# Attention stage of a two-layer backbone: a third buffer of probabilities, and another order of work on the scalar and the vector engine

## Chip, cores and metric

The kernel runs on one core of one Trainium2 chip. The metric is the device time of one execution in microseconds (us); the time given for a kernel is the median of its runs. The engines are named as in the profile: PE (TensorE, matrix multiplies; PEld is its loading of weights), ACT (ScalarE), DVE (VectorE), POOL (GpSimd), SP (SyncE, which issues most DMAs). Each engine works through its own queue of instructions in order. An instruction can wait until a semaphore has reached a value, and then everything behind it on the same engine waits too.

## The reference, cut to what matters

The program computes two layers over 512 latent tokens with 256 context tokens, width 1024, in fp32. Layer 0 is attention with 8 query heads and 2 key/value heads of width 128 and then a squared-ReLU MLP; layer 1 is a Hyena long convolution and an MLP. Only the attention is touched:

```python
def gqa_attend(q, k, v):
    s = jnp.einsum('bqkgd,bskd->bkgqs', q, k).astype(jnp.float32) * (q.shape[-1] ** -0.5)
    p = jax.nn.softmax(s, axis=-1).astype(v.dtype)
    return jnp.einsum('bkgqs,bskd->bqkgd', p, v)
...
    k_all = jnp.concatenate([k_l, k_c], axis=1)     # 512 latent + 256 context keys
    v_all = jnp.concatenate([v_l, v_c], axis=1)
    o = lax.map(lambda qblk: gqa_attend(qblk, k_all, v_all), qb)   # 4 blocks of 128 queries
```

## The kernel before, in words

Every large product is made at nearly fp32 accuracy from three faster products: each operand is split into a high part (a copy in the rounded format fp32r) and a low part (value minus high part), and `mm3` (L1430 to L1434) adds high times high, high times low and low times high. So each operand costs a copy on ACT (high part) and a subtraction on DVE (low part).

The attention is cut into NQ = 32 tiles: 8 heads times 4 blocks of 128 queries, each against NK = 768 keys. Each engine has its own loop over steps n, and a step works on several tiles at once, each at another stage of its life. With the names used below, step n holds:

- On PE (L1583 to L1610), in this order: **T(n-3)**, six 128x128 transposes of the normalised probabilities of tile n-3 into PSUM (L1589); **S(n)**, the scores of tile n, two `mm3` of 512 and 256 columns; and at odd n from 5 on **PV**, `prob_values((n-5)/2)`, 18 matmuls of 256 columns that multiply two tiles of turned probabilities with the values.
- On ACT (L774 to L800): at even n from 6 on **O**, the high part of the attention output, which waits for PV (L778); **H(n-3)**, the high part `phi` of the turned probabilities, which waits for T(n-3) (L785); and **B(n-1)** and **E(n-1)**, a small scaling of the negated row maximum (L794) and the exponential from PSUM into `PROB`, with the row sums into `rsum` (L795). They wait for the maximum of tile n-1, and for the transposes of the tile that used this buffer of `PROB` before.
- On DVE (L1190 to L1216): **R(n-2)** and **N(n-2)**, the reciprocal of the row sum and the normalisation of the probabilities in place (L1196, L1197), which wait for E(n-2); **L(n-3)**, the low part `plo` of the turned probabilities, which waits for H(n-3) (L1202); **M(n)**, the row maximum of the scores of tile n, which waits for S(n) (L1208); at even n from 6 on the low part of the attention output (L1181); and at n = 3, 7, 11, ... one row of the modulation product of 128x1024 elements (**A**, L1187), 8 in all.

Scores and turned probabilities share three double banks of PSUM in rotation. `score(n)` is double bank (2n+1) mod 3 and `turned(m)` is 2(m+3) mod 3, so T(n-3) is written where the scores of tile n-2 were, and S(n) where the turned probabilities of tile n-4 were. PE therefore has these waits ahead of T(n-3) and S(n):

```python
                    pe.wait_ge(p_done, m + 1)               # m = n - 3: N(n-3)
                    pe.wait_ge(exp_done, min(n - 1, NQ))    # E(n-2) has read the scores
                    ...
                    if n >= 4:
                        pe.wait_ge(plo_done, n - 3)         # L(n-4) has read the turned tile
```

`PROB` has two buffers in `scratch` (`S[:, 0:2]` and `S[:, 2:4]`), used by tile number modulo 2.

Of the kernel before, what the change touches and what calls it, by code (L numbers as in the profile page):

```python
# [27 lines left out]
ALU = mybir.AluOpType  # L28
ACT = mybir.ActivationFunctionType
AX = mybir.AxisListType  # L30

P = 128
# [4 lines left out]
NK = NT + NC  # L37
# [51 lines left out]
def build(nc, xT, ctxT, cT, cols, wpack, ahead, apack, fw1, fw2, fw3, featsT, decay, tables, consts, ropes, fdram, out):  # L89
    with ExitStack() as ctx:  # L90
        def sb(name, shape, dt=F32, stack=ctx):
            return stack.enter_context(nc.sbuf_tensor(name, shape, dt))

        def sem(name):
            return ctx.enter_context(nc.semaphore(name))
# [14 lines left out]
        S = sb("scratch", [P, 12, NT])  # L110
# [5 lines left out]
        gain = sb("gain", [P, 2, 4, KC])  # L116
        gainc = sb("gainc", [P, KC])
        nmax = sb("nmax", [P, 2])
        rsum = sb("rsum", [P, 2])
        rinv = sb("rinv", [P, 2])  # L120
        asum = sb("asum", [P, ADA_QUARTER])
        qg = sb("qg", [P, 1])
        rq = sb("rq", [P, NH * QT])
        bmax = sb("bmax", [P, 2])
        epst = sb("eps", [P, 1])
        tap2 = sb("tap2", [P, 2, NT])
        ident, ones = (cst[:, n, :] for n in range(2))
# [108 lines left out]
        rq_done = sem("rq_done")  # L236
# [11 lines left out]
        score_done = sem("score_done")  # L248
        nmax_done = sem("nmax_done")
        exp_done = sem("exp_done")  # L250
        rinv_done = sem("rinv_done")
        p_done = sem("p_done")
        pt_done = sem("pt_done")
# [81 lines left out]
        def spread(a):  # L335

            return TRIO[a % 3][:, :, :].rearrange("p a b -> p (a b)")[:, 0:NK]

        def score(n):

            return spread(2 * n + 1)

        def turned(m):

            return spread(2 * (m + 3))
# [6 lines left out]

        XH = [S[:, 4 + j % 4, :] for j in range(KC)]
        YC = [y[:, j, :] for j in range(KC)]
        PROB = [S[:, 2 * n:2 * n + 2, :].rearrange("p a b -> p (a b)")[:, 0:NK] for n in range(2)]

        FP, FP_, FQ, FQ_ = (araw[:, n // 2, n % 2 * NT:(n % 2 + 1) * NT] for n in range(4))
        UNIT_RAW = (es[:, 0, :], tap2[:, 0, :])
# [8 lines left out]
        NQ = NH * QT  # L367
# [7 lines left out]
        def f(ap):  # L375
            return ap.bitcast(F32)
# [261 lines left out]
        def _(act):  # L638
            own = Own(act, own_act)
            A = nc.scalar.activation  # L640
# [133 lines left out]
            for n in range(NQ + 5):  # L774
                if n >= 6 and n % 2 == 0:
                    m = (n - 6) // 2
                    act.wait_ge(pv_done, m + 1)
                    A(hhi[:, m // 2, (m % 2) * 2 * P:(m % 2 + 1) * 2 * P], (B2, B3)[m % 2][:, 0:2 * P],  # L778
                      ACT.Copy).then_inc(ohi_done, 1)
                m = n - 3  # L780
                if 0 <= m < NQ:
                    act.wait_ge(pt_done, m + 1)
                    if m >= 4:
                        act.wait_ge(pv_done, m // 2 - 1)
                    A(phi[:, m // 2 % 2, :, (m % 2) * P:(m % 2 + 1) * P],  # L785
                      turned(m).rearrange("p (b c) -> p b c", b=KT), ACT.Copy).then_inc(phi_done, 1)
                m = n - 1
                if 0 <= m < NQ:
                    act.wait_ge(nmax_done, m + 1)
                    if m >= 2:  # L790
                        act.wait_ge(pt_done, m - 1)
                    if m == 0:
                        act.wait_ge(rq_done, 1)
                    own(A(bmax[:, m % 2:m % 2 + 1], nmax[:, m % 2:m % 2 + 1], ACT.Copy, scale=rq[:, m:m + 1]))  # L794
                    A(PROB[m % 2], score(m), ACT.Exp, bias=bmax[:, m % 2:m % 2 + 1], scale=rq[:, m:m + 1],  # L795
                      accum_out=rsum[:, m % 2:m % 2 + 1]).then_inc(exp_done, 1)
                if n == 1:
                    act.wait_ge(csum_done, 1)
                    A(crow[:, 0:NT], B2[:, :], ACT.Copy).then_inc(crow_done, 1)
                    A(crow[:, NT:2 * NT], B3[:, :], ACT.Copy).then_inc(crow_done, 1)  # L800
# [112 lines left out]
            for k in range(4):  # L913
                z_hi(k)
                n = 4 * (k + 1)
# [47 lines left out]
        def _(dve):  # L963
            own = Own(dve, own_dve)
            TT = nc.vector.tensor_tensor
            STT = nc.vector.scalar_tensor_tensor
            TS = nc.vector.tensor_scalar
# [135 lines left out]
            for q in range(4):  # L1103
                for ft in range(2):
                    n = 4 * q + 2 * ft
# [72 lines left out]
            def o_lo(m):  # L1178
                dve.wait_ge(ohi_done, m + 1)
                cols_ = slice((m % 2) * 2 * P, (m % 2 + 1) * 2 * P)  # L1180
                TT(hlo[:, m // 2, cols_], (B2, B3)[m % 2][:, 0:2 * P], f(hhi[:, m // 2, cols_]), ALU.subtract).then_inc(olo_done, 1)  # L1181

            def ada_row(k, loads, dst, early=False):

                dve.wait_ge(arow_in[k], 16 * loads)
                slot = arow_slot(k, early)
                nc.vector.tensor_tensor_reduce(slot, slot, crow if early else crow1[:, :], 1.0, 0.0, ALU.mult, ALU.add,  # L1187
                                               dst).then_inc(arow_done, 1)

            for n in range(NQ + 5):  # L1190
                m = n - 2
                if 0 <= m < NQ:
                    dve.wait_ge(exp_done, m + 1)
                    if m >= 2:
                        dve.wait_ge(p_done, m - 1)
                    own(nc.vector.reciprocal(rinv[:, m % 2:m % 2 + 1], rsum[:, m % 2:m % 2 + 1]))  # L1196
                    TS(PROB[m % 2], PROB[m % 2], rinv[:, m % 2:m % 2 + 1], None, ALU.mult).then_inc(p_done, 1)  # L1197
                m = n - 3
                if 0 <= m < NQ:
                    dve.wait_ge(phi_done, m + 1)  # L1200
                    at = slice((m % 2) * P, (m % 2 + 1) * P)
                    TT(plo[:, m // 2 % 2, :, at], turned(m).rearrange("p (b c) -> p b c", b=KT),  # L1202
                       f(phi[:, m // 2 % 2, :, at]), ALU.subtract).then_inc(plo_done, 1)
                if n < NQ:
                    dve.wait_ge(score_done, n + 1)
                    if n >= 2:
                        dve.wait_ge(exp_done, n - 1)
                    nc.vector.tensor_reduce(out=nmax[:, n % 2:n % 2 + 1], in_=score(n), op=ALU.max,  # L1208
                                            axis=AX.X, negate=True).then_inc(nmax_done, 1)
                if n >= 6 and n % 2 == 0:  # L1210
                    o_lo((n - 6) // 2)
                if n < NQ and n % 4 == 3:
                    r = n // 4
                    if r == 0:
                        dve.wait_ge(crow_done, 2)
                    ada_row(r % ADA_RING, r // ADA_RING + 1, mods[:, 16 + r:17 + r], True)  # L1216
# [156 lines left out]
            for k in range(5):  # L1373
# [4 lines left out]
                n = 4 * (k + 1)  # L1378
# [48 lines left out]
        def _(pe):  # L1427
            mm = nc.tensor.matmul

            def mm3(o, lh, ll, rh, rl, first, last):  # L1430

                mm(o, lh, rh, start=first, stop=False)  # L1432
                mm(o, lh, rl, start=False, stop=False)  # L1433
                return mm(o, ll, rh, start=False, stop=last)  # L1434
# [148 lines left out]
            for n in range(NQ + 4):  # L1583
                m = n - 3
                if 0 <= m < NQ:
                    pe.wait_ge(p_done, m + 1)
                    pe.wait_ge(exp_done, min(n - 1, NQ))
                    for kt in range(KT):
                        ins = nc.tensor.transpose(turned(m)[:, kt * P:(kt + 1) * P],  # L1589
                                                  PROB[m % 2][:, kt * P:(kt + 1) * P], ident)  # L1590
                    ins.then_inc(pt_done, 1)
                if n < NQ:
                    h, qt = divmod(n, QT)
                    g = h // GROUP
                    if n == 0:
                        pe.wait_ge(job_lo, len(JOBS))
                    if n == 1:
                        pe.wait_ge(vlo_done, 2 * NKV)
                    if n >= 4:
                        pe.wait_ge(plo_done, n - 3)  # L1600
                    w = slice(qt * P, (qt + 1) * P)
                    mm3(score(n)[:, 0:NT], ghi[:, h, w], glo[:, h, w], khi[:, g, 0:NT], klo[:, g, 0:NT], True, True)
                    mm3(score(n)[:, NT:NK], ghi[:, h, w], glo[:, h, w], khi[:, g, NT:NK], klo[:, g, NT:NK],
                        True, True).then_inc(score_done, 1)
                if n == 1:
                    pe.wait_ge(cdiag_done, KC)
                    mm(B2[:, :], ones, S[:, 4, :], start=True, stop=True)
                    mm(B3[:, :], ones, S[:, 5, :], start=True, stop=True).then_inc(csum_done, 1)
                if n >= 5 and n % 2 == 1:
                    prob_values((n - 5) // 2)  # L1610
# [91 lines left out]
            for k in range(5):  # L1702
                if k < 4:
                    transposes(k)
                n = 4 * (k + 1)
# [119 lines left out]
```

## Time and profile before

| | before |
|---|---|
| median of 3 runs | 1568.01 us (1565.47 to 1570.09) |
| the profiled execution | 1570.97 us, its span 1569.2 us |
| PE busy, share of the span | 1377.1 us, 88% |
| DVE busy | 959.4 us, 61% |
| ACT busy | 615.3 us, 39% |
| POOL busy | 171.4 us, 11% |
| mean granted clock of TensorE | 0.942 of full speed |

The span runs from the first to the last instruction of the execution that was profiled; 1.8 us of that execution lie around it. The shares are means over stages with different limits. The attention loop is a small stage: scores of tile 0 start at 242.1 us, and the last matmuls of PV end at about 367 us, 8% of the span. A row of the timeline gives start, duration, engine, line, operation, output<-input tile and shape, how many instructions were merged (x6), and in brackets how long the engine had been idle before it and what released it. PSUM tiles are called `bank`; `PROB` is part of `scratch`. The ends of matmuls are modelled by the profiler.

### The profile page before, as it was taken

What the parts mean: (1) busy time and instruction counts of PE and PEld (TensorE: products, weight loads), DVE (VectorE), ACT (ScalarE), POOL (GpSimd) and SP (SyncE); (2) the same over time, 40 slices, a digit from 0 to 9 for tenths busy, and PEclk for the clock granted to TensorE, in tenths of its full rate; (3) what the DMA queues carried; (4) which work ended last, traced back from release to release, by engine and by line L of the source; (5) the groups of instructions that cost most, each with busy time, mean ns of one, the idle gap of its engine ahead of it and who ended that gap; (6) DMA issues with size and microseconds to landing.
All of it is one profiled execution on the core that took longest, in us unless ns stands there. A gap on an engine that the chain in (4) does not pass through costs nothing. (4 is left out here: it accounts for less than half of the span.)

```text
span 1569.2 us, 17367 instructions
## 1 busy us (share of the span) xinstructions
PE 1377.1 (88%) x6214; PEld 1091.4 (70%) x6214; DVE 959.4 (61%) x1262; ACT 615.3 (39%) x929; POOL 171.4 (11%) x150
## 2 busy tenths in 40 slices
PE   7997997888679999999958787888876999999995
PEld 1455786777458888888836676777754888888884
DVE  5786786886965555555567778877537333333344
ACT  2234545663344342534324334233324435243430
POOL 0503220002510000000330000000142000000022
PEclk9998999999879999999978988989997999999998
DMA  8443332105626565565211122121220322223221
GB/s 332 146 173 121 109 113 89 32 23 183 206 70 203 185 198 193 186 205 179 94 54 66 56 93 81 67 68 41 90 71 27 108 94 94 94 94 107 94 80 54
DMA packets 47373, 179.34 MB, mean 114 GB/s; under 512 B 6007, under 2 KB 6263, under 8 KB 43800
## 3 DMA queue, kind: packets, MB, share of 16 engines
q1 hardware_dynamic: 44312, 165.55, 31.3%
q0 software_dynamic: 3008, 13.11, 2.6%
q8 instruction: 30, 0.49, 0.1%
q14 instruction: 23, 0.19, 0.0%
HBM read 165.53 MB, written 10.49 MB: 112 GB/s over the span
## 5 line engine op out<-in xcount | busy, mean ns | idle before, releaser
L1432 PE MATMUL bank<-hhi,whi 128*128 128x512 f32 x864 | 343.6, 398 | 34.8 <-DVE hlo L985 22.4
L1434 PE MATMUL bank<-hhi,wlo 128*128 128x512 f32 x864 | 339.9, 393 | 0.0
L1433 PE MATMUL bank<-hlo,whi 128*128 128x512 f32 x864 | 339.8, 393 | 0.0
L972 DVE TENSOR_TENSOR wlo<-raw,whi 128x1024 fp32r<-128x1024 f32 x180 | 234.8, 1307 | 67.9 <-ACT whi L647 65.4
L1432 PE MATMUL bank<-ghi,whi 128*128 128x512 f32 x576 | 224.9, 390 | 4.6 <-DVE glo L1371 4.6
L1433 PE MATMUL bank<-glo,whi 128*128 128x512 f32 x576 | 224.5, 390 | 0.0
L1434 PE MATMUL bank<-ghi,wlo 128*128 128x512 f32 x576 | 224.5, 390 | 0.0
L1432 PEld LDWEIGHTS bank<-hhi,whi 128*128 128x128 f32 x864 | 164.2, 190 | 81.3 <-issue 30.6
L647 ACT ACTIVATE whi<-raw 128x1024 fp32r<-128x1024 f32 x180 | 188.6, 1050 | 6.4 <-DMA raw<-in_wpack 5.6
L1434 PEld LDWEIGHTS bank<-hhi,wlo 128*128 128x128 f32 x864 | 164.3, 190 | 34.8
L1433 PEld LDWEIGHTS bank<-hlo,whi 128*128 128x128 f32 x864 | 164.6, 190 | 32.6
L1249 DVE TENSOR_TENSOR glo<-scratch,ghi 128x512 fp32r<-128x512 f32 x64 | 44.4, 693 | 185.5 <-ACT ghi L850 185.5
L1260 DVE TENSOR_TENSOR scratch<-scratch 128x512 f32<-128x512 f32 x64 | 44.3, 692 | 174.4 <-ACT scratch L858 174.4
L858 ACT ACTIVATE scratch<-bank 128x512 f32<-128x512 f32 x64 | 38.3, 598 | 241.4 <-PE bank L1434 241.4
L1432 PEld LDWEIGHTS bank<-ghi,whi 128*128 128x128 f32 x576 | 108.5, 188 | 27.7 <-DVE glo L1371 5.0
L1433 PEld LDWEIGHTS bank<-glo,whi 128*128 128x128 f32 x576 | 108.6, 188 | 22.5
L1434 PEld LDWEIGHTS bank<-ghi,wlo 128*128 128x128 f32 x576 | 108.4, 188 | 22.5
L594 POOL TENSOR_TENSOR scratch<-scratch 128x512 f32<-128x512 f32 x32 | 37.4, 1168 | 771.1 <-DVE scratch L1260 644.6
L846 ACT ACTIVATE scratch<-bank 128x512 f32<-128x512 f32 x64 | 38.3, 598 | 168.5 <-PE bank L1434 168.5
L1624 PE MATMUL bank<-scratch,consts 128*128 128x512 f32 x24 | 24.8, 1138 | 40.9 <-POOL scratch L605 40.9
L911 ACT ACTIVATE ghi<-scratch 128x512 fp32r<-128x512 f32 x24 | 14.7, 631 | 96.6 <-DVE scratch L1337 96.6
L597 POOL TENSOR_TENSOR scratch<-scratch 128x512 f32<-128x512 f32 x24 | 49.0, 2041 | 1.9
(250 smaller groups left out, 2072.6 us busy)
## 6 DMA issues: line engine op xcount, KB each, us to landing
raw<-in_wpack SPq DMA_DIRECT2D x180, 512.0 KB, 3.4
araw<-in_apack SPq DMA_DIRECT2D x40, 512.0 KB, 3.4
amore<-in_apack SPq DMA_DIRECT2D x36, 512.0 KB, 3.3
ablk<-in_ahead SPq DMA_DIRECT2D x8, 1024.0 KB, 8.6
spectra<-scratch SPq DMA_DIRECT2D x8, 1024.0 KB, 4.2
araw<-spectra POOLq DMA_DIRECT2D x8, 1024.0 KB, 5.1
fs<-in_decay SPq DMA_DIRECT2D x8, 256.0 KB, 3.7
scratch<-in_decay SPq DMA_DIRECT2D x8, 256.0 KB, 3.0
```

Of the source, the lines that this page charges most:

```text
L594: ins = nc.gpsimd.tensor_tensor(dst, y[:, j, :], y[:, j, :], ALU.mult)
L597: ins = nc.gpsimd.tensor_tensor(S[:, 11, :], S[:, 11, :], S[:, 10, :], ALU.add)
L647: A(whi[:, s, :], raw[:, r, :], ACT.Copy).then_inc(hi_done, 1)
L846: A(S[:, 8 + j % 2, :], AB[:, j % 2, :], ACT.Relu).then_inc(evac_done, 1)
L858: A(S[:, 8 + j % 2, :], AB[:, j % 2, :], ACT.Copy).then_inc(evac_done, 1)
L972: TT(wlo[:, s, :], raw[:, r, :], f(whi[:, s, :]), ALU.subtract).then_inc(lo_done, 1)
L1249: TT(glo[:, j, :], S[:, 10 + j % 2, :], f(ghi[:, j, :]), ALU.subtract).then_inc(g_done, 1)
L1260: TT(y[:, j, :], y[:, j, :], S[:, 8 + j % 2, :], ALU.add).then_inc(y_done, 1)
L1432: mm(o, lh, rh, start=first, stop=False)
L1433: mm(o, lh, rl, start=False, stop=False)
L1434: return mm(o, ll, rh, start=False, stop=last)
L1624: mm(B2[:, :], ones, y[:, 2 * i, :], start=i == 0, stop=i == KC // 2 - 1).then_inc(ss_done, 1)
```

## The change

`PROB` gets a third buffer (`S[:, 4:6]`), and `rsum` and `rinv` a third column; tiles use them modulo 3. The exponential of tile m then waits for the transposes of tile m-3 instead of m-2, and the normalisation for that of tile m-3 instead of m-2.

On ACT, B(n-1) and E(n-1) now stand ahead of H(n-3) in each step. On DVE, M(n) now stands ahead of L(n-3). PE's order and its waits stay as they are, apart from the buffer that the transposes read.

```diff
-        rsum = sb("rsum", [P, 2])
-        rinv = sb("rinv", [P, 2])
+        rsum = sb("rsum", [P, 3])
+        rinv = sb("rinv", [P, 3])
...
-        PROB = [S[:, 2 * n:2 * n + 2, :].rearrange("p a b -> p (a b)")[:, 0:NK] for n in range(2)]
+        PROB = [S[:, 2 * n:2 * n + 2, :].rearrange("p a b -> p (a b)")[:, 0:NK] for n in range(3)]
...
+                m = n - 1
+                if 0 <= m < NQ:
+                    act.wait_ge(nmax_done, m + 1)
+                    if m >= 3:
+                        act.wait_ge(pt_done, m - 2)
+                    if m == 0:
+                        act.wait_ge(rq_done, 1)
+                    own(A(bmax[:, m % 2:m % 2 + 1], nmax[:, m % 2:m % 2 + 1], ACT.Copy, scale=rq[:, m:m + 1]))
+                    A(PROB[m % 3], score(m), ACT.Exp, bias=bmax[:, m % 2:m % 2 + 1], scale=rq[:, m:m + 1],
+                      accum_out=rsum[:, m % 3:m % 3 + 1]).then_inc(exp_done, 1)
                 m = n - 3
                 if 0 <= m < NQ:
                     act.wait_ge(pt_done, m + 1)
...
-                m = n - 1
-                if 0 <= m < NQ:
-                    act.wait_ge(nmax_done, m + 1)
-                    if m >= 2:
-                        act.wait_ge(pt_done, m - 1)
...
                 m = n - 2
                 if 0 <= m < NQ:
                     dve.wait_ge(exp_done, m + 1)
-                    if m >= 2:
-                        dve.wait_ge(p_done, m - 1)
...
+                    if m >= 3:
+                        dve.wait_ge(p_done, m - 2)
...
+                if n < NQ:
+                    dve.wait_ge(score_done, n + 1)
+                    if n >= 2:
+                        dve.wait_ge(exp_done, n - 1)
+                    nc.vector.tensor_reduce(out=nmax[:, n % 2:n % 2 + 1], in_=score(n), op=ALU.max,
+                                            axis=AX.X, negate=True).then_inc(nmax_done, 1)
                 m = n - 3
                 if 0 <= m < NQ:
                     dve.wait_ge(phi_done, m + 1)
...
-                if n < NQ:
-                    dve.wait_ge(score_done, n + 1)
-                    if n >= 2:
-                        dve.wait_ge(exp_done, n - 1)
-                    nc.vector.tensor_reduce(out=nmax[:, n % 2:n % 2 + 1], in_=score(n), op=ALU.max,
-                                            axis=AX.X, negate=True).then_inc(nmax_done, 1)
...
-                                                  PROB[m % 2][:, kt * P:(kt + 1) * P], ident)
+                                                  PROB[m % 3][:, kt * P:(kt + 1) * P], ident)
```

## Rows read from the trace of the kernel before

**Rows 1.** The first line of the page.
```profile
span 1569.2 us, 17367 instructions
```

**Rows 2.** Busy time by stretch: window, its length, busy us (instructions), PEclk, DMA share, GB/s.
```profile
290.28:353.24 62.96, 51.72 (x381) 47.84 (x380) 52.87 (x89) 40.82 (x81) 0.00 (x0) 1.00 0.08 26
353.24:363.41 10.17, 5.99 (x38) 5.54 (x37) 5.52 (x11) 4.47 (x8) 0.57 (x1) 0.83 0.18 53
```

**Rows 3.** Waits from 246 to 366 us: engine, line <- releaser: us in total, times, longest.
```profile
PE bank L1589 <- ACT scratch L795: 23.9, 17, 2.9
ACT phi L785 <- PE bank L1589: 21.7, 32, 1.2
DVE plo L1202 <- ACT phi L785: 19.1, 30, 3.2
```

**Rows 4.** Timeline, PE, two steps of the steady loop (T, S, T, S, PV, T).
```profile
290.28 0.82 PE L1589 MATMUL bank<-consts,scratch 128*128 128x128 f32 x6
290.85 0.48 PE L1432 MATMUL bank<-khi,ghi 128*128 128x512 f32 x1
...
291.85 0.28 PE L1434 MATMUL bank<-khi,glo 128*128 128x256 f32 x1
...
293.38 0.85 PE L1589 MATMUL bank<-consts,scratch 128*128 128x128 f32 x6 [1.25 <-ACT scratch L795]
...
293.99 0.48 PE L1432 MATMUL bank<-khi,ghi 128*128 128x512 f32 x1
...
295.12 0.28 PE L1432 MATMUL bank<-phi,vhi 128*128 128x256 f32 x1
...
297.29 0.82 PE L1589 MATMUL bank<-consts,scratch 128*128 128x128 f32 x6
```

**Rows 5.** Timeline, ACT, the even step of the same two (O, H, B, E).
```profile
290.47 0.38 ACT L778 ACTIVATE hhi<-bank 128x256 fp32r<-128x256 f32 x1 [1.09 <-PE bank L1434]
...
291.13 0.81 ACT L785 ACTIVATE phi<-bank 128x768 fp32r<-128x768 f32 x1 [0.27 <-PE bank L1589]
...
291.84 0.28 ACT L794 ACTIVATE bmax<-nmax,rq 128x1 f32<-128x1 f32 x1
...
292.15 0.99 ACT L795 ACTIVATE scratch<-bank,bmax,rq 128x768 f32<-128x768 f32 x1
...
293.05 0.19 ACT L795 ACTIVATION_READ_ACCUMULATOR scratch<-bank,bmax,rq 128x1 f32 x1
```

**Rows 6.** Timeline, DVE, the odd step (low part of output, R, N, L, M, A).
```profile
293.71 0.42 DVE L1181 TENSOR_TENSOR hlo<-bank,hhi 128x256 fp32r<-128x256 f32 x1
...
294.04 0.15 DVE L1196 RECIPROCAL rinv<-rsum 128x1 f32<-128x1 f32 x1
...
294.23 0.62 DVE L1197 TENSOR_SCALAR scratch<-scratch,rinv 128x768 f32<-128x768 f32 x1
...
295.11 0.96 DVE L1202 TENSOR_TENSOR plo<-bank,phi 128x768 fp32r<-128x768 f32 x1 [0.26 <-ACT phi L785]
...
295.99 0.94 DVE L1208 TENSOR_REDUCE nmax<-bank 128x1 f32<-128x768 f32 x1
...
296.85 1.21 DVE L1187 CUSTOM_DVE_ANT_0 scratch<-scratch 128x1024 f32<-128x1024 f32 x1
```

**Rows 7.** Timeline, behind the last tile: L and the PV that waits for it.
```profile
362.40 0.96 DVE L1202 TENSOR_TENSOR plo<-bank,phi 128x768 fp32r<-128x768 f32 x1 [3.19 <-ACT phi L785]
...
363.41 0.39 PE L1432 MATMUL bank<-phi,vhi 128*128 128x256 f32 x1 [1.89 <-DVE plo L1202]
```

**Rows 8.** Timeline, PE, first matmuls of S(3) and S(5), in the filling of the loop.
```profile
252.70 0.48 PE L1432 MATMUL bank<-khi,ghi 128*128 128x512 f32 x1
...
258.97 0.48 PE L1432 MATMUL bank<-khi,ghi 128*128 128x512 f32 x1
```

**Rows 9.** Timeline, PE, the emptying: first matmul of PV at step 33, then T(31).
```profile
357.02 0.56 PE L1432 MATMUL bank<-phi,vhi 128*128 128x256 f32 x1
...
360.70 0.82 PE L1589 MATMUL bank<-consts,scratch 128*128 128x128 f32 x6
```

More of the change, by code:

```diff
@@ L786, in _ @@
                       turned(m).rearrange("p (b c) -> p b c", b=KT), ACT.Copy).then_inc(phi_done, 1)
-                m = n - 1
-                if 0 <= m < NQ:
-                    act.wait_ge(nmax_done, m + 1)
-                    if m >= 2:
-                        act.wait_ge(pt_done, m - 1)
[L792 to L796, printed above, removed]
                 if n == 1:
@@ L1193, in _ @@
                     dve.wait_ge(exp_done, m + 1)
-                    if m >= 2:
-                        dve.wait_ge(p_done, m - 1)
-                    own(nc.vector.reciprocal(rinv[:, m % 2:m % 2 + 1], rsum[:, m % 2:m % 2 + 1]))
-                    TS(PROB[m % 2], PROB[m % 2], rinv[:, m % 2:m % 2 + 1], None, ALU.mult).then_inc(p_done, 1)
+                    if m >= 3:
+                        dve.wait_ge(p_done, m - 2)
+                    own(nc.vector.reciprocal(rinv[:, m % 3:m % 3 + 1], rsum[:, m % 3:m % 3 + 1]))
+                    TS(PROB[m % 3], PROB[m % 3], rinv[:, m % 3:m % 3 + 1], None, ALU.mult).then_inc(p_done, 1)
+                if n < NQ:
[4 more added lines that the diff above has]
+                                            axis=AX.X, negate=True).then_inc(nmax_done, 1)
                 m = n - 3
```

## The prediction

> **What bounds the kernel now.** The change touches only the attention loop, so I read that stage alone: first the busy times of its stretches, then its waits, then two steps of the timeline, engine by engine. From 290.28 to 353.24 us the loop goes round nine pairs of steps at full granted clock, 2.4 GHz; 62.96 / 9 = 7.00 us a pair. PE is busy for 51.72 us of it, and no other engine is busier than 52.87 us [rows 2]. So no engine is full, and a circle of waits must set the pace. The waits name three links of it: transposes wait for the exponential (17 times, 23.9 us in total), the high part for the transposes, the low part for the high part [rows 3].
>
> The timeline of one pair closes the circle. The even step starts with T at 290.28 and goes on with S at 290.85. H can start when the transposes are in PSUM, at 291.13; B follows at 291.84, E at 292.15, and the next T starts at 293.38, released by E [rows 4, 5]. That is 0.85 + 0.71 + 0.31 + 1.23 = 3.10 us, of which PE idles 1.25. In the odd step PE runs T, S and PV without a gap: T to S 0.61, S to PV 1.13, PV to the next T 2.17, together 3.91 [rows 4]. 3.10 + 3.91 = 7.01. The reader should see two things: E of the even step sits behind H, which waits for T; and the odd step is PE's own work, which no change of order on ACT and DVE can shorten. Counted from S to S, the even step gives 3.14 (290.85 to 293.99) and the odd one 0.57 + 3.30 = 3.87.
>
> PE's work in a pair is 2 x 0.57 + 2 x 1.13 + 2.17 = 5.57 us, so at most 7.00 - 5.57 = 1.43 us a pair is there to win.
>
> **The change, part by part.**
>
> *Third buffer.* It costs no work and adds none. Alone it loosens the wait of E(n-1) from T(n-3) to T(n-4). With E moved ahead of H this is needed: otherwise E would still wait for the same transposes.
>
> *E ahead of H on ACT.* In the even step E no longer waits for T. Count from the start of S of the even step, S_e = 0 (290.85). O starts at -0.38 and takes 0.38 [rows 5], so B can start at 0.00; the maximum it needs is from the odd step before and long done. Exactly how soon a queued ACT instruction starts behind another is bounded by two ends: H to B took 0.71 with an H of 0.81, an overlap of 0.10, so B starts between -0.10 and 0.00. E starts 0.31 later, at 0.21 to 0.31, and PE may go on with T 1.23 later, at 1.44 to 1.54 instead of at 2.53. This part of the old circle opens by 1 us. N, which T also needs, is of an older tile and done.
>
> *M ahead of L on DVE, and what it does to S.* This is the step that decides. PE's S(n) waits for L(n-4), since it writes into the bank that L reads. L(n-4) belongs to DVE's step n-1. Until now it stood ahead of M(n-1) there; now it stands behind, and M(n-1) cannot start before S(n-1) is complete. So a new circle arises: S(n-1), M(n-1), L(n-4), S(n). Its length:
> - S to M. The last matmul of S starts 1.00 after the first and is shown as 0.28 long [rows 4]. ACT started H 0.03 after the shown end of the transposes (290.28 + 0.82 = 291.10, H at 291.13). The trace has no maximum that waited for scores in the steady loop, so I take the same 0.03: 1.00 + 0.28 + 0.03 = 1.31. Bounds: 1.28 (no release time) and 1.36.
> - M to L. In the trace L comes first: L to M 0.88, and M to A 0.86 [rows 6]. I take the pitch behind a maximum, 0.86. L's own condition, H, is looked at below.
> - L to S. Only the last PV shows a wait for L that nothing else covers: L at 362.40, PE at 363.41, 1.01 us [rows 7].
>
> Sum 1.31 + 0.86 + 1.01 = 3.18 us from S to S, in every step. In the odd step PE needs 3.87 of its own, so the circle is hidden there. In the even step PE needs only 1.13 + 0.57 = 1.70, or by T's earliest start 1.54 + 0.61 = 2.15, and waits for L until 3.18. Before, this step took 3.14. So the new pair is 3.18 + 3.87 = 7.05 us against 7.00: the wait for the exponential is replaced by a wait for the low part of nearly the same length. 13 pairs (n = 6 to 31) give 13 x 0.05 = +0.7 us.
>
> *H behind E.* L of the even step also needs H, which now waits for E. The accumulator is read 0.90 after E's start and takes 0.19 [rows 5], so H starts between 0.21 + 0.99 = 1.20 and 0.31 + 1.09 = 1.40, and L may start 0.84 after it (its 0.81 [rows 5] and the same 0.03), at 2.04 to 2.24. M's turn gives 1.31 + 0.86 = 2.17. So H just fits on the near end and is 0.07 late on the far end, 13 x 0.07 = 0.9 us more. I take the near end, since queued instructions in rows 5 and 6 do overlap; the far end goes into the range.
>
> *Room for A and the rest of DVE.* Behind L of the odd step (S_o + 2.17) stand L 0.88, A at most 1.21, R 0.19 and N 0.62 [rows 6]: free at S_o + 5.07. M of the next even step can start at S_o + 3.87 + 1.31 = 5.18. A still fits, by 0.1 us. In the filling it doesn't. There is no PV at step 3, so M(4) could start at S(3) + 3.18 + 1.31 = 4.49, but A holds DVE until 5.07: 0.58 late with full lengths, 0.4 with overlaps. S(3) to S(5) took 6.27 [rows 8] and will take 2 x 3.18 + 0.5 = 6.86: +0.6 us.
>
> *Emptying.* At step 32 E(31) comes ahead of H(29), and T(30) can start about 1 us earlier. But PV of step 33 needs L(29), which needs H(29) behind that E: this PV starts where it did. It ran at 1.2 GHz: clock 0.83 in this stretch [rows 2], 360.70 - 357.02 = 3.7 us instead of 2.17 [rows 4, 9]. The old gap ahead of T(30) is now cut in two by T. If the granted clock stays up, 1.5 us are won; if it falls as before, nothing. I take nothing and keep 1.5 for the range.
>
> *Other costs.* The third columns of `rsum` and `rinv` move later tensors by 8 bytes; no row tells a price. Work behind the loop is as before and starts when the last PV does.
>
> **How the numbers follow.** +0.7 + 0.6 + 0.0 = +1.3 us, on 1570.97 us of the profiled execution: 1572.3. That execution lies 2.96 us above the median of the runs shown (its span is 1569.2 [rows 1]). The forecast for the median is 1568.0 + 1.3 = 1569.3. Its own range is -1.5 (the clock in the emptying) to +1.6 (late H 0.9, slow release of M 13 x 0.05), 1567.8 to 1570.9; the shown runs scatter by about 2.3 us to each side, a median of them by less, which I take as 1.5: 1566.3 to 1572.4. I give it 0.75: 0.70 within 0.3% (4.7 us, about what a measurement of this kernel tells from no change), 0.03 faster, 0.02 slower.
>
> **The rivals.**
>
> *The exponential was the only brake (faster).* If L doesn't hold S back, the pair falls until DVE is full: 2 x (0.19 + 0.62 + 0.88 + 0.86) + 0.33 + 1.21 / 2 = 6.04 us [rows 6]. That is 13 x 0.96 = 12.5 us less, 1555.5. For it speaks that the waits name E first; against it the wait of PE for `plo_done` and the order on DVE, which leave no way round. Between the two, each 0.1 us that S, M and L are shorter than I think gives only 1.3 us. Chance 0.08.
>
> *H late behind E (slower).* ACT has O, B and E ahead of H in the even step, and H's L then holds S. It decides once H starts later than S_e + 1.33. If O is released 0.2 us later than now or E holds ACT for its full length and a wait besides, L is late by up to 0.3, a pair takes 7.35 and the loop 13 x 0.35 = 4.6 us more: with the filling 1573.2. Nothing in rows 5 shows such a delay. Chance 0.08, half of it over 0.3%.
>
> *The clock (slower).* PE's idle time in a pair, 1.25 us in one piece, becomes two pieces of about 0.3 and 1.1. If the granted clock fell in the steady loop as it does in the emptying, each PV would cost 1.5 us more [rows 4, 9]; seen in half of the pairs this is +10 us, 1579. Against it: the total idle time is the same and the clock stood at 1.00 [rows 2]. Chance 0.05.
>
> *A maximum that blocks DVE longer (slower).* If L cannot start at once behind M but DVE first empties, for at most once more the length of M, L starts 1.9 instead of 0.86 behind M, and the pair grows by 1.0: 13 x 1.04 + 1.3 = +14.8 us, 1583. Rows 6 speak against it: 0.88 from L to M and 0.86 from M to A, both less than the durations shown. Chance 0.04. The Trainium skill (VectorE: DVE Perf Modes, "The DRAIN you can't avoid") has such a rule: after each instruction the engine drains for about its duration less 266 ns before the next one starts. By it M to L would be 0.94 + 0.68 = 1.62, an estimate from that page, and the time 1579. The trace doesn't agree, since 0.86 to 0.88 was measured.
>
> **Chances and range.** Faster by over 0.3%: 0.03 + 0.08 = 0.11. Slower: 0.02 + 0.04 + 0.05 + 0.04 = 0.15. Within: 0.74. The range 1564.5 to 1573.5 leaves out the faster rival and most of the last two, under 0.2.
>
> **What would show it.** In the profile after: the wait of transposes for the exponential in even steps falls from 1.25 to about 0.3 us, and S of odd steps (n odd) shows a new wait of about 1 us for `plo`, some 13 times; M no longer starts behind L but 1.3 us behind S; a pair still takes 7.0 to 7.1 us. It would be wrong if pairs take less than 6.9 us, if S doesn't wait for `plo`, or if L starts later than 0.9 us behind M.

## The result

The changed kernel takes 1573.38 us (median of 6 runs, 1571.39 to 1574.57) beside 1567.78 us of the kernel before (6 runs). The ratio is 1.0030 with a 95% interval of 1.0017 to 1.0043: +5.6 us between the medians, +2.7 to +6.7 us by the interval. It was measured a second time (label e_again, below): 1572.45 against 1568.97 us, ratio 1.0016, interval 1.0003 to 1.0029. The two intervals overlap between 1.0017 and 1.0029. So the change costs the kernel some 0.2 to 0.3 per cent and gains nothing. The forecast was +1.3 us.

The profiled execution of the changed kernel took 1572.57 us:

```profile
span 1570.8 us, 17365 instructions
```

Waits in the attention loop, 246 to 370 us (engine, line <- releaser: us in total, times, longest). They answer to [rows 3]. In the changed kernel L788 is the exponential E, L795 the high part H, L1202 the maximum M and L1208 the low part L:

```profile
PE bank L1432 <- DVE plo L1208: 15.8, 17, 1.9
DVE nmax L1202 <- ACT scratch L788: 8.9, 12, 1.3
DVE nmax L1202 <- PE bank L1434: 8.6, 16, 1.9
PE bank L1589 <- ACT scratch L788: 6.2, 15, 2.8
...
DVE plo L1208 <- ACT phi L795: 3.0, 2, 2.1
...
ACT phi L795 <- PE bank L1589: 0.6, 2, 0.3
```

The three waits of [rows 3] are nearly gone: 23.9 to 6.2 us for the transposes behind the exponential, 21.7 to 0.6 for H, 19.1 to 3.0 for L. In their place PE waits for L, 17 times and 15.8 us: 15 times ahead of scores and twice ahead of the last two PVs. DVE's maximum waits for scores. (In even steps the profile names L788, the exponential, for this wait. But M(n) needs only the exponential of tile n-2, and the reciprocal R(n-2) ahead of it on DVE has already waited for that one. The exponential that ends at this moment is that of tile n-1. So the scores are what releases M. In e_dve_only below, M starts the same 1.32 us behind the scores and the profile names the scores.)

One pair of steps on PE, as [rows 4] before (T, S, T, S, PV, T):

```profile
291.38 0.82 PE L1589 MATMUL bank<-consts,scratch 128*128 128x128 f32 x6
291.95 0.48 PE L1432 MATMUL bank<-khi,ghi 128*128 128x512 f32 x1
...
292.96 0.28 PE L1434 MATMUL bank<-khi,glo 128*128 128x256 f32 x1
293.40 0.85 PE L1589 MATMUL bank<-consts,scratch 128*128 128x128 f32 x6 [0.17 <-ACT scratch L788]
295.15 0.51 PE L1432 MATMUL bank<-khi,ghi 128*128 128x512 f32 x1 [0.90 <-DVE plo L1208]
...
296.31 0.28 PE L1432 MATMUL bank<-phi,vhi 128*128 128x256 f32 x1
...
298.48 0.82 PE L1589 MATMUL bank<-consts,scratch 128*128 128x128 f32 x6
```

The same even step on ACT and DVE (O, B, E, H; M, L), as [rows 5, 6]:

```profile
291.58 0.39 ACT L778 ACTIVATE hhi<-bank 128x256 fp32r<-128x256 f32 x1 [2.29 <-PE bank L1434]
291.86 0.28 ACT L787 ACTIVATE bmax<-nmax,rq 128x1 f32<-128x1 f32 x1
292.18 0.99 ACT L788 ACTIVATE scratch<-bank,bmax,rq 128x768 f32<-128x768 f32 x1
...
293.16 0.80 ACT L795 ACTIVATE phi<-bank 128x768 fp32r<-128x768 f32 x1
...
293.27 0.96 DVE L1202 TENSOR_REDUCE nmax<-bank 128x1 f32<-128x768 f32 x1 [1.30 <-ACT scratch L788]
294.14 0.95 DVE L1208 TENSOR_TENSOR plo<-bank,phi 128x768 fp32r<-128x768 f32 x1
```

The transposes now start 1.45 us behind the even scores instead of 2.53. But the odd scores start only at 295.15, 3.20 us behind the even ones: M begins 1.32 us after S, L 0.87 after M, S 1.01 after L. That is the circle the prediction worked out at 3.18. The pair takes 298.48 - 291.38 = 7.10 us, against 7.00 before. Every pair from S(6) to S(30) takes this, 7.08 to 7.11 us.

### The profile page after: what moved, and what is told of

Its sections match the earlier page's. It is cut to its first block and busy times, and to the rows that moved or that the text cites. A ratio compares the mean times of both kernels' runs of the same rounds, so it can differ in the third digit from the quotient of the medians.

```text
span 1570.8 us, 17365 instructions
## 1 busy us (share of the span) xinstructions
PE 1383.9 (88%) x6214; PEld 1093.1 (70%) x6214; DVE 956.9 (61%) x1262; ACT 613.9 (39%) x929; POOL 172.0 (11%) x150
## 5 line engine op out<-in xcount | busy, mean ns | idle before, releaser
L1433 PEld LDWEIGHTS bank<-glo,whi 128*128 128x128 f32 x576 | 108.5, 188 | 22.6
L911 ACT ACTIVATE ghi<-scratch 128x512 fp32r<-128x512 f32 x24 | 14.7, 631 | 96.7 <-DVE scratch L1337 96.7
```

## The experiments

The theory, theory A below: in steps without PV the circle S, M, L, S sets the pace, and the exponential ahead of the high part frees time that nothing can use. All medians and ratios are against runs of the kernel before on the same chip.

| label | what | median, before beside it (us) | ratio, 95% interval | pair (us) |
|---|---|---|---|---|
| e_again | the changed kernel again | 1572.45, 1568.97 | 1.0016, 1.0003 to 1.0029 | 7.10 |
| e_buffers | third buffer and columns alone | 1569.43, 1568.97 | 1.000, 0.999 to 1.001 | 7.00 |
| e_dve_only | M ahead of L alone | 1570.81, 1568.97 | 1.0013, 1.000 to 1.0025 | 7.09 |
| e_act_only | buffers, E ahead of H alone | 1585.43, 1568.97 | 1.0098, 1.0081 to 1.0115 | 8.17 (mean of 13), 8.00 at full clock |
| e_longer_circle | changed kernel, one link more | 1576.21, 1569.07 | 1.0041, 1.0027 to 1.0054 | 7.43 |
| e_mixed | order by even and odd step | 1555.36, 1569.07 | 0.9912, 0.9898 to 0.9925 | 6.29 |
| e_mixed_out_early | the same, O ahead of E | 1570.81, 1569.07 | 1.0002, 0.9989 to 1.0014 | 6.94 |
| p_mixed | e_mixed again | 1556.26, 1568.17 | 0.9921, 0.9906 to 0.9935 | 6.28 |

### The changed kernel again

> The changed kernel once more, beside the parts of it. Theory A (the loop alone pays: scores, maximum, low part, scores is the circle that binds in steps without PV): pair of steps 7.10 us, the profiled span 1 to 2 us over that of before, and the rest of the first measured +5.6 us is scatter of runs, so the median comes out +1 to +3 us. Theory B (something outside the loop's order costs some 4 us too, such as later tensors moved by the third columns): +5 to +6 us again.

Measured +3.5 us between the medians, +0.5 to +4.6 by the interval, with a span of 1570.7 us, 1.5 more than before's. That is a little above theory A's range, and the interval leaves theory B's +5 to +6 out; theory B is tested better by the next run.

### Buffers and columns alone

Part of the diff on the kernel before (the waits and the other uses of the buffers and columns change with it, as in the changed kernel):

```diff
-        PROB = [S[:, 2 * n:2 * n + 2, :].rearrange("p a b -> p (a b)")[:, 0:NK] for n in range(2)]
+        PROB = [S[:, 2 * n:2 * n + 2, :].rearrange("p a b -> p (a b)")[:, 0:NK] for n in range(3)]
...
-                    TS(PROB[m % 2], PROB[m % 2], rinv[:, m % 2:m % 2 + 1], None, ALU.mult).then_inc(p_done, 1)
+                    TS(PROB[m % 3], PROB[m % 3], rinv[:, m % 3:m % 3 + 1], None, ALU.mult).then_inc(p_done, 1)
```

> Three buffers of probabilities and three columns of sums, but both orders as before. Theory A: nothing waits for a buffer in before, so the pair stays 7.00 us and the median within 1 us of before. Theory B: +4 us with a pair of 7.00 us.

Ratio 1.000, pair 7.00 us, the transposes wait for the exponential as before (17 times, 22.6 us). The buffers and the shifted tensors cost nothing and bring nothing, to within the interval of 1.6 us either way; theory B falls. What the change costs, its two new orders cost.

### Each order alone

On the vector engine alone, two buffers (as a diff on the kernel before):

```diff
-                m = n - 3
-                if 0 <= m < NQ:
-                    dve.wait_ge(phi_done, m + 1)
...
                     nc.vector.tensor_reduce(out=nmax[:, n % 2:n % 2 + 1], in_=score(n), op=ALU.max,
                                             axis=AX.X, negate=True).then_inc(nmax_done, 1)
+                m = n - 3
+                if 0 <= m < NQ:
+                    dve.wait_ge(phi_done, m + 1)
...
```

> Two buffers, the scalar engine in its old order, on the vector engine the maximum ahead of the low part. Theory A: the same circle of scores, maximum and low part holds the scores of odd steps 3.20 us behind those of even steps, and the transposes that wait for the exponential are ready 0.6 us earlier than that, so the pair is 7.10 us as in the changed kernel: the exponential's new place brings nothing beside it. Median +1 to +2 us. Rival (the exponential behind the high part adds to the low part's wait): pair over 7.3 us, +4 us or more.

```profile
291.32 0.48 PE L1432 MATMUL bank<-khi,ghi 128*128 128x512 f32 x1
...
292.64 0.96 DVE L1202 TENSOR_REDUCE nmax<-bank 128x1 f32<-128x768 f32 x1 [1.29 <-PE bank L1434]
...
293.52 0.95 DVE L1208 TENSOR_TENSOR plo<-bank,phi 128x768 fp32r<-128x768 f32 x1
...
293.86 0.85 PE L1589 MATMUL bank<-consts,scratch 128*128 128x128 f32 x6 [1.25 <-ACT scratch L795]
...
294.52 0.50 PE L1432 MATMUL bank<-khi,ghi 128*128 128x512 f32 x1
```

The transposes wait for the exponential until 293.86, as before the change (L795 is still the exponential here), and end just when L releases the scores at 294.52: S to S is 3.20 us again, 291.32 to 294.52. So this order alone gives the pair of the changed kernel, and the two waits are almost equally late in it, 0.06 us apart. The expectation put the transposes 0.6 us ahead; that was wrong, for the six transposes themselves take 0.6 and had been left out there. So this run alone can't tell which of the two waits binds; that is left to the run with one link more. The median, +1.8 us (interval 0 to +3.9), is as theory A said, and the rival's pair of over 7.3 us is refuted.

On the scalar engine alone, three buffers, DVE in its old order (as a diff on the changed kernel):

```diff
-                if n < NQ:
-                    dve.wait_ge(score_done, n + 1)
...
                     TT(plo[:, m // 2 % 2, :, at], turned(m).rearrange("p (b c) -> p b c", b=KT),
                        f(phi[:, m // 2 % 2, :, at]), ALU.subtract).then_inc(plo_done, 1)
+                if n < NQ:
+                    dve.wait_ge(score_done, n + 1)
...
```

> Three buffers, exponential ahead of the high part on the scalar engine, the vector engine in its old order (low part ahead of maximum). Theory A, by the same way of counting: a circle through both engines in every step, low part to maximum 0.88, maximum to scaling 1.00, to exponential 0.32, to high part 0.98, to low part 0.84: 4.0 us a step, 8.05 a pair, 13 pairs of +1.05 us: +13 to +15 us. Rival (the exponential was the only brake, as the waits of before name it): a pair of 6.0 to 6.9 us, 2 to 12 us less than before.

Two steps, DVE and ACT (M, B, E, H, L; here L1208 is M and L1202 is L):

```profile
289.98 0.96 DVE L1202 TENSOR_TENSOR plo<-bank,phi 128x768 fp32r<-128x768 f32 x1 [0.31 <-ACT phi L795]
290.85 0.95 DVE L1208 TENSOR_REDUCE nmax<-bank 128x1 f32<-128x768 f32 x1
...
291.83 0.29 ACT L787 ACTIVATE bmax<-nmax,rq 128x1 f32<-128x1 f32 x1 [1.89 <-DVE nmax L1208]
...
292.16 0.99 ACT L788 ACTIVATE scratch<-bank,bmax,rq 128x768 f32<-128x768 f32 x1
...
293.14 0.80 ACT L795 ACTIVATE phi<-bank 128x768 fp32r<-128x768 f32 x1
293.98 0.96 DVE L1202 TENSOR_TENSOR plo<-bank,phi 128x768 fp32r<-128x768 f32 x1 [1.12 <-ACT phi L795]
```

L to L is 4.00 us round M, B, E and H, as worked out (4.0), and it is the same in steps where the output copy stands first on ACT. From the output copy at 262.05 to that at 368.30 us there are 26 such turns; 21 of them take 4.00 us, a pair 8.00. The other five take 4.44 to 4.47, and the reason is the clock. Five times in this loop (at about 274, 291, 315, 332 and 356 us) TensorE's granted clock falls to 1.2 GHz for some 3 us. The PV under way ends later, the output copy waits for it, and E and H stand behind the copy:

```profile
293.25 0.41 PE L1432 MATMUL bank<-phi,vhi 128*128 128x256 f32 x1
...
296.01 0.39 ACT L778 ACTIVATE hhi<-bank 128x256 fp32r<-128x256 f32 x1 [2.06 <-PE bank L1434]
...
298.42 0.96 DVE L1202 TENSOR_TENSOR plo<-bank,phi 128x768 fp32r<-128x768 f32 x1 [1.90 <-ACT phi L795]
```

In the other traces the granted clock stays at 1.00 from 263 us to the emptying. Here PE had waited 1.41 and 0.39 us in the step in which the clock fell. So the 13 pairs cost 13.0 us at full clock and 2.2 us by the low clock, 15.2 us together, and the projection starts at half clock in this trace (below), 1.6 us. That makes 16.8 us beside the measured +16.5 (interval +12.7 to +18.0). The rival is refuted with the sign reversed: the exponential that the waits of before name first is worth +16 us when it alone is put first. So the two moves belong together: exponential first makes the high part depend on the newest maximum; only with the maximum ahead of the low part does this not turn into a circle through both engines.

### One link more in the circle

A diff on the changed kernel:

```diff
                                             axis=AX.X, negate=True).then_inc(nmax_done, 1)
+                if n >= 6 and n % 2 == 0:
+                    o_lo((n - 6) // 2)
                 m = n - 3
...
-                if n >= 6 and n % 2 == 0:
-                    o_lo((n - 6) // 2)
```

> The changed kernel with one more link in the circle: in even steps the low part of the attention output (0.33 us of the vector engine's time) stands between the maximum and the low part of the probabilities instead of behind both. The engine does the same work in the same step. Theory A (scores, maximum, low part, scores binds in even steps): the scores of odd steps come 0.33 us later, 3.53 us behind those of even steps, pair 7.43 us, 13 pairs: +4.3 us on the changed kernel, +6 to +8 us on the kernel before. Rival (some other wait binds and the low part only ends near it): less than +1 us on the changed kernel.

```profile
293.57 0.48 PE L1432 MATMUL bank<-khi,ghi 128*128 128x512 f32 x1
...
295.03 0.85 PE L1589 MATMUL bank<-consts,scratch 128*128 128x128 f32 x6 [0.16 <-ACT scratch L788]
297.11 0.50 PE L1432 MATMUL bank<-khi,ghi 128*128 128x512 f32 x1 [1.24 <-DVE plo L1210]
```

297.11 - 293.57 = 3.54 us, 0.34 more than in the changed kernel, while the transposes stay at +1.46. The pair is 7.43 us, the median 1576.21, +2.8 and +3.8 us on the two medians of the changed kernel (+4.3 expected). The link is worth its full length, so this circle is the one that binds.

### Orders chosen by step

If the circle S, M, L is hidden in odd steps (PE needs 3.9 us there) and binds in even ones, each step should have its own order. The blocks O, H, E of ACT and M, L of DVE are made functions of n (`att_out`, `att_hi`, `att_exp`, `att_max`, `att_lo`), otherwise as in the changed kernel; in odd steps `att_out` does nothing:

```diff
+                for part in ((att_out, att_hi, att_exp) if n % 2 else (att_exp, att_out, att_hi)):
+                    part(n)
...
+                for part in ((att_max, att_lo) if n % 2 else (att_lo, att_max)):
+                    part(n)
```

> Three buffers, and the order chosen by step. Even steps (no PV covers): scalar engine exponential, output, high part; vector engine low part ahead of maximum. Odd steps (PV covers): scalar engine high part, exponential; vector engine maximum ahead of low part. Theory A: the exponential of an even step then starts when the maximum of the odd step is done, before PV ends; high part 0.5 to 0.8 us and low part 1.3 to 1.6 us behind the start of the even scores, so the odd scores follow them after 2.3 to 2.6 us instead of 3.14; pair 6.25 (no modulation row) to 6.5 us (with one), 13 pairs of -0.5 to -0.75: -7 to -10 us on the kernel before. Rival (the loop cannot go below 7 us a pair because the engines' latencies bind whatever the order): within 1 us of before.

One pair, PE first (T, S, T, S, T), then the even step on ACT and DVE. Line numbers are of this kernel: L1598 T, L1441 the first product, L789 E, L778 O, L797 H, L1195 L, L1188 M:

```profile
283.33 0.82 PE L1598 MATMUL bank<-consts,scratch 128*128 128x128 f32 x6
283.91 0.48 PE L1441 MATMUL bank<-khi,ghi 128*128 128x512 f32 x1
...
285.05 0.81 PE L1598 MATMUL bank<-consts,scratch 128*128 128x128 f32 x6
286.22 0.50 PE L1441 MATMUL bank<-khi,ghi 128*128 128x512 f32 x1 [0.36 <-DVE plo L1195]
...
289.55 0.82 PE L1598 MATMUL bank<-consts,scratch 128*128 128x128 f32 x6
```

```profile
283.12 0.99 ACT L789 ACTIVATE scratch<-bank,bmax,rq 128x768 f32<-128x768 f32 x1
...
284.10 0.37 ACT L778 ACTIVATE hhi<-bank 128x256 fp32r<-128x256 f32 x1
284.37 0.81 ACT L797 ACTIVATE phi<-bank 128x768 fp32r<-128x768 f32 x1
285.21 0.96 DVE L1195 TENSOR_TENSOR plo<-bank,phi 128x768 fp32r<-128x768 f32 x1 [0.86 <-ACT phi L797]
...
286.08 0.95 DVE L1188 TENSOR_REDUCE nmax<-bank 128x1 f32<-128x768 f32 x1
```

E starts 0.79 us ahead of the even scores, L 1.30 behind them, and the odd scores follow 2.31 us behind the even ones instead of 3.14 before. With a modulation row in the pair before it is 2.49 (290.12 to 292.61). Four pairs take 302.12 - 276.95 = 25.17 us, 6.29 each, inside the expected 6.25 to 6.5. The median falls by 13.7 us, ratio 0.9912; expected were 7 to 10 us. 13 pairs of 0.71 are 9.2 us; the tables of stretches below show where more is. The same kernel measured again:

> The mixed order again. Its first measurement gave -13.7 us, of which its pairs of steps (6.29 instead of 7.00 us, 13 pairs) carry 9.2, and filling and emptying 2.3 (first maximum to projection 109.0 instead of 120.6 us at full clock). If the loop is the whole cause: -11 to -12 us on the kernel before, and the first maximum starts between 243 and 246 us as in the others. If something outside the loop gained too: -13 to -15 us again, with the first maximum before 243 us.

-11.9 us between the medians, ratio 0.9921, interval 0.9906 to 0.9935 (-14.7 to -10.2 us), which reaches into both expected ranges. The first maximum at 243.41 us decides nothing either, since it starts between 241.8 and 246.0 us in the traces of kernels with the same work ahead of the loop. What places the gain in the loop are the stretches below. This version is faster than both kernels.

The same with `(att_out, att_exp, att_hi)` in even steps:

> As the mixed order, but with the high part of the output ahead of the exponential in even steps, as in the kernel before: the exponential then waits for PV again. Theory A: exponential 0.2 us, high part 1.1 us, low part 1.95 us behind the even scores, odd scores after 2.97 us, pair 6.85 us, 13 pairs of -0.15: -2 us on the kernel before, so most of the mixed order's gain hangs on taking the exponential out from behind PV. Rival (the gain comes from the vector engine's order alone): same as the mixed order, -7 us or more.

```profile
290.82 0.38 ACT L778 ACTIVATE hhi<-bank 128x256 fp32r<-128x256 f32 x1 [1.25 <-PE bank L1443]
...
291.20 0.48 PE L1441 MATMUL bank<-khi,ghi 128*128 128x512 f32 x1
...
293.24 0.96 DVE L1195 TENSOR_TENSOR plo<-bank,phi 128x768 fp32r<-128x768 f32 x1 [1.60 <-ACT phi L797]
...
294.25 0.50 PE L1441 MATMUL bank<-khi,ghi 128*128 128x512 f32 x1 [0.76 <-DVE plo L1195]
```

With the output copy first, everything on ACT waits for PV; L starts 2.04 us behind the scores and the odd scores 3.05. The pair is 6.94 us (276.75 to 283.69 to 290.63), 0.06 less than before and 0.09 more than expected, and the median doesn't differ from before (the expected -2 us lies just outside the interval). So nearly the whole gain of e_mixed hangs on one more move, which neither kernel has: the exponential out from behind PV. That the move is needed is shown; that it would be enough is not, since it wasn't run in the changed kernel, where the circle S, M, L of 3.20 us would still stand.

### Where the clock falls

> A second trace of the kernel before, to see where TensorE's granted clock falls. Its first trace has a PV of the emptying at 1.2 GHz (3.7 instead of 2.2 us) and full clock where the output projection starts. Theory C (where the clock falls is luck of the execution): the PV at 1.2 GHz, or the start of the projection, or neither, with any order of work. Theory D (it hangs on the order of work): the same as in the first trace.

> A third trace of the changed kernel. In its first two the output projection starts at 1.2 GHz, which costs 1.9 us between its first matmul and the first scaling behind it (50.6 and 50.7 instead of 48.7 us). Theory D (it hangs on the order of work): 50.6 again. Theory C (luck): 48.7 or 50.6. From the first maximum to the first matmul of the projection 122.4 us in both, or 124 with a slow PV.

> A fourth trace of the changed kernel, with the same expectations: theory D 50.6 us from the first matmul of the output projection to the first scaling, theory C 48.7 or 50.6.

Three stretches from each trace, in us; all times are starts read from the timeline:

| trace | first M | first M to projection | projection to the first small product on `gain` | last two together |
|---|---|---|---|---|
| before | 246.00 | 122.36 | 48.71 | 171.07 |
| p_before | 242.94 | 123.01 | 48.74 | 171.75 |
| e_buffers | 244.15 | 120.55 | 48.72 | 169.27 |
| after | 245.52 | 122.53 | 50.62 | 173.15 |
| e_again | 245.43 | 122.33 | 50.71 | 173.04 |
| p_after_1 | 244.32 | 122.96 | 50.54 | 173.50 |
| p_after_2 | 241.76 | 121.64 | 48.73 | 170.37 |
| e_dve_only | 244.16 | 122.54 | 48.71 | 171.25 |
| e_longer_circle | 245.74 | 127.64 | 48.74 | 176.38 |
| e_mixed_out_early | 245.58 | 122.46 | 48.75 | 171.21 |
| e_act_only | 244.98 | 138.70 | 50.34 | 189.04 |
| e_mixed | 242.36 | 109.00 | 48.75 | 157.75 |
| p_mixed | 243.41 | 110.17 | 48.75 | 158.92 |

In before and p_before both PVs of the emptying run at 1.2 GHz, that of step 33 [rows 9] and the last one: from the one to the other and on to the projection it takes 11.3 us, in e_buffers, with the same order of work and full clock, 8.4. That is 1.4 and 1.5 us. Three of four traces of the changed kernel have the PV of step 33 and the first half of the last one at full clock, and then the end of the last PV (0.6 to 0.8 us longer) and the start of the projection (1.9 us) at 1.2 GHz:

```profile
366.18 0.41 PE L1432 MATMUL bank<-phi,vhi 128*128 128x256 f32 x1
...
368.05 0.76 PE L1432 MATMUL bank<-hhi,whi 128*128 128x512 f32 x1 [1.02 <-DVE hlo L1181]
...
369.46 0.63 PE L1432 MATMUL bank<-hhi,whi 128*128 128x512 f32 x1
```

The fourth, p_after_2, does not:

```profile
363.40 0.47 PE L1432 MATMUL bank<-hhi,whi 128*128 128x512 f32 x1 [1.03 <-DVE hlo L1181]
...
364.17 0.40 PE L1432 MATMUL bank<-hhi,whi 128*128 128x512 f32 x1
```

So theory D, in its strict form, falls: whether the clock is low there changes between executions of one kernel. When it is low, it is so at the same place in all three traces of the changed kernel, and in both of the kernel before at another. With four traces of the changed kernel and three of the old order it can't be said whether the order of work shifts the odds.

The same traces, split further, as means in us. The old order is before, p_before and e_buffers; S(n) is the first matmul of the scores of tile n:

| stretch | old order (3) | changed (4) | mixed (2) |
|---|---|---|---|
| first M to S(6) | 17.47 | 18.08 | 17.12 |
| S(6) to S(30), 12 pairs | 83.96 | 85.20 | 75.38 |
| S(30) to the PV of step 33 | 10.22 | 10.15 | 8.70 |
| that PV to the last PV | 5.89 | 4.96 | 4.96 |
| last PV to the projection | 4.44 | 3.98 | 3.44 |
| projection to the small product | 48.72 | 50.15 | 48.75 |
| together | 170.70 | 172.51 | 158.34 |

The changed kernel is +1.8 us: +1.2 in the pairs and +0.6 in the filling. The clock takes no part in it on balance: the changed kernel has 1.4 us less in the two rows of the last PVs and 1.4 us more in the projection. (The filling differs by 1.2 us among the three traces of the old order, so its +0.6 is a mean within that scatter.) Between the two traces without low clock here, e_buffers and p_after_2, the difference is +1.1; between those with it, +1.8.

The mixed order is -12.4 us, which agrees with the runs, -11.9 and -13.7: -8.6 in the 12 pairs, -1.5 from S(30) to the PV of step 33, -0.4 in the filling, and -1.9 in the two rows of the last PVs. The last 1.9 us don't come from shorter circles: the mixed traces need the same 8.4 us there as e_buffers, and the mean of the old order holds two traces with slow PVs. So the order itself is worth 10.5 us by these traces.

## Why the prediction was right

*The signs.* Those that the prediction named all came: the transposes' wait for the exponential in even steps fell from 1.25 to 0.17 us (0.3 forecast), scores of odd steps wait 0.9 us for L in all 13 pairs, M starts 1.32 us behind S, and a pair takes 7.10 us. None of those that would have shown it wrong did.

*What bounds the kernel.* Right. The circle through H, E and T read from [rows 4, 5] was there. Taking E out from behind H moved T from 2.53 to 1.45 us behind the scores, 1.44 to 1.54 predicted.

*The new circle.* Right, and nearly to the number: 1.31 + 0.86 + 1.01 = 3.18 predicted, 1.32 + 0.87 + 1.01 = 3.20 measured. The release of a maximum by scores, which the trace of before did not show, was taken from the transposes and H, 0.03 us; measured, the maximum starts 0.03 us after the last score matmul's shown end (292.96 + 0.28 = 293.24, M at 293.27). That the circle binds is shown by e_longer_circle. In e_dve_only the pair is the same without the exponential's move, but there the transposes' wait lies within 0.06 us of it.

*The odd step.* Taken as 3.87 us, PE's own work as before; it is 3.90 (295.15 to 299.05). Scores behind a wait are slower at the start: their first matmul is shown with 0.51 instead of 0.48 us, and PV follows S after 1.16 instead of 1.13. With the circle's 0.02 the pair is 7.10, not 7.05: 13 x 0.10 = 1.3 us in the pairs instead of 0.7. This is the term that was mis-sized. The slow start can be read from the trace before: behind the wait of 1.25 us the transposes are shown with 0.85 instead of 0.82 us and the scores follow them after 0.61 instead of 0.57 [rows 4]. The prediction counted it in the even step and left it out where its own new wait would put it.

*H behind E.* Right at the near end: H starts 1.21 us behind the scores (1.20 predicted), ends at 293.96, and L at 294.14 is not late.

*Room for A, and the filling.* Right. In the loop A leaves 0.18 us (the maximum at 286.18 waited that long; predicted 0.1). In the filling A holds the maximum of step 4, and it starts 3.61 us behind that of step 3. From M(3) to M(5), both released by their scores, it is 6.83 us; from S(3) to S(5) before took 6.27 [rows 8], and 6.86 was predicted:

```profile
254.19 0.96 DVE L1202 TENSOR_REDUCE nmax<-bank 128x1 f32<-128x768 f32 x1 [1.89 <-PE bank L1434]
...
257.80 0.95 DVE L1202 TENSOR_REDUCE nmax<-bank 128x1 f32<-128x768 f32 x1
...
261.02 0.96 DVE L1202 TENSOR_REDUCE nmax<-bank 128x1 f32<-128x768 f32 x1 [0.68 <-PE bank L1434]
```

*Emptying.* PV of step 33 starts where it did, bound by L: 10.15 us behind S(30), 10.22 before. The clock had more at stake than the 1.5 us that the prediction took from this PV: the last PV ran at 1.2 GHz too, which [rows 9] did not show, together 2.9 us. In three traces of four the changed kernel won 2.1 to 2.3 us of them (by comparison with before and p_before) and paid 1.9 us some 9 us later, where the projection starts at half clock. That the low clock could reappear in the stage behind was not foreseen; the forecast said work behind the loop is as before. That it took nothing for the clock came out right in the mean, by luck.

*The sum.* +1.3 us forecast; with the pair at its measured size, 1.3 + 0.6 = +1.9; the traces show +1.8. The runs show +4.7 us by the first ratio and +2.5 by the second, with intervals that reach down to +2.7 and +0.5. What the runs have beyond the traces' +1.8, if it is real, stays open. The executions that were traced differ by +2.1 us in the mean (1571.3 and 1569.2). From the small product to the end, before and the changed kernel's first trace have the same 1152.1 us (1569.2 - 417.07, 1570.8 - 418.67), and before the loop the work is the same, though the first maximum starts up to 4 us apart in the traces. So the mechanism was right and the number came close from below: 1573.38 us lies above the prediction's own inner range (to 1572.4) and 0.1 us inside the stated one (to 1573.5). With runs that scatter by 1.5 us to each side, that it fell inside was partly luck.

*The rivals.* The exponential as the only brake: refuted, most plainly by e_act_only. Late H: not seen. The clock in the steady loop: not seen in the changed kernel; e_act_only shows that it can fall there, and that it then costs 0.45 us each time, since most of the slower PV is covered. A maximum that blocks DVE longer: L follows M after 0.87 us, less than the 0.96 shown for M. So the drain that the Trainium skill states (VectorE: DVE Perf Modes, "The DRAIN you can't avoid") does not hold L back here. That section has an exception, which the prediction left out: "A next op that is not held starts earlier".

## What to carry to other kernels

A wait that the profile names is one link; before an operation is moved away from it, write down the circle that closes it and the circle that the moved operation joins, and compare their lengths: here 3.14 us gave way to 3.20. The exponential first in even steps only, and there ahead of the output copy as well, with the maximum first in odd steps only, gave 12 us, 10.5 of them by the shorter loop. In a software pipeline whose steps differ in length, the best order of work can differ by step as well.

## What the runs showed of the hardware

The stretch at 1.2 GHz near the end of the loop comes in some executions of a kernel and not in others (three traces of four of the changed kernel). Where it came it cost 2.6 to 3.0 us in all: 1.4 and 1.5 us on the two last PVs, or 0.6 to 0.8 us on the last one and 1.9 us on the start of the projection. One trace of each kernel can therefore differ by over 2 us for that reason alone, more than this change does.

A low clock costs only what nothing covers. In e_act_only it fell five times under a PV in the steady loop and each time lengthened the turn of 4.00 us by 0.45.

TensorE starts more slowly out of a wait, even a short one: after 0.9 us of idle time its first 512-column matmul is shown with 0.51 us instead of 0.48, and the work behind it comes 0.03 us later, 13 times in this loop.
